# The order of two-expert and three-expert passes in a mixture-of-experts round

## The chip, the cores and the metric

The kernel runs on one core of one Trainium2 chip. The metric is the device time of one execution in microseconds (us). Times of the kernel before: 1380.34, 1383.5 and 1382.48 us, median 1382.48 us.

## What is computed

One inference step of a trunk of two layers over 256 tokens (128 context tokens, 128 latent tokens) of width 1024. Layer 0 mixes tokens with a bidirectional gated recurrence, layer 1 with differential attention; each is followed by a mixture of experts with 64 experts of width 256, of which each token takes 8. Everything is float32. The part that the change touches, cut from the reference:

```python
def moe(x, router, router_bias, w_gate, w_up, w_down, ws_gate, ws_up, ws_down):
    scores = jax.nn.sigmoid(x.astype(jnp.float32) @ router.astype(jnp.float32))
    ...
    h = jax.nn.silu(jnp.einsum('btd,edf->btef', x, w_gate)) * jnp.einsum('btd,edf->btef', x, w_up)
    routed = jnp.einsum('btef,efd->btd', h * combine[..., None].astype(x.dtype), w_down)
    shared = (jax.nn.silu(x @ ws_gate) * (x @ ws_up)) @ ws_down
    return routed + shared
```

What is left out picks 8 of the 64 experts for each token (within 4 of 8 groups); combine holds their weights and is zero elsewhere.

## The kernel before

**Passes.** Tokens are gathered per expert. A pass works on 128 rows of gathered tokens, cut into four blocks of 32. `SUBS` (line 60) says which of the pass's experts each block belongs to: kind A has two experts of 64 rows, kind B three (64, 32, 32), kind D two (96, 32). The experts are ranked by how many tokens chose them; `column_ranks` (line 67) gives three-block places to the fullest, two-block places to the middle, one-block places to the emptiest. There are 26 passes in a layer: passes 0 and 1 (kind A, experts 0 to 3) and three rounds of eight, whose kinds `BODY` (line 54) spells out: 2 + 3 x 8 = 26 passes and 4 + 3 x 20 = 64 experts. "Expert n" here means the n-th in the order of the passes.

**One pass on TensorE** (`one_pass`, from line 1343): `gate_up` (128 rows against the gate and up projections, all of the pass's experts side by side on the array), the first half of the scatter of the pass before, the turning of the hidden rows, the second half of that scatter, the gather for the next pass, `down` (hidden rows against the down projections, called here the down products), and `turn_slots` for the next pass. Passes 4, 11 and 19 carry in addition a piece of the shared expert. Pass 25, the last, takes gate and up apart: first the gate half, then both scatters, then the up half, then its down products. After it, layer 0 sums mod_w columns (`sum_mod(16)`), which needs a load of its own.

**Weights.** An expert has three loads: gate and up (1 MB each) and down (1 MB). Gate and up go into one of six places (`GATE_SLOTS`, line 50), expert n into place n mod 6; down into one of five (`DOWN_SLOTS`), expert n into place n mod 5. In the profile's names, places 0 to 3 are in `ring`, the others in `W`. Which load may follow which pass is set by two lists (lines 469 and 470):

```python
GATES_FREED = [[n + GATE_SLOTS for n in experts_of(p) if n + GATE_SLOTS < E] for p in range(PASSES)]
DOWNS_FREED = [[n + DOWN_SLOTS for n in experts_of(p) if n + DOWN_SLOTS < E] for p in range(PASSES)]
```

**The queue of loads.** SyncE issues all of them, in this order for every pass (`refill`, line 577; the first pass and the last three experts, whose gate and up are split, are left out here):

```python
eng.wait_ge(s.gu_done, done)
for n, e in gates:
    load_gate_up(gate_place(n % GATE_SLOTS), a["moe_w_gate"][L, e], a["moe_w_up"][L, e], gate_loaded(n))
eng.wait_ge(s.down_done, 2 * done)
for n, e in expert_ids(DOWNS_FREED[p]):
    load_down(down_place(n % DOWN_SLOTS), a["moe_w_down"][L, e], sem[f"down{n % DOWN_SLOTS}_loaded"])
```

So the gates that pass p frees are loaded once its gate and up products are done (line 554), the downs that it frees once its down products are done (line 557), and SyncE goes on to pass p+1 only then. On TensorE, line 1199 waits for the gate and up loads of the pass, line 1208 for its down loads.

Of the kernel before, what the change touches and what calls it, by code (L numbers as in the profile page):

```python
# [50 lines left out]
GATE_LOADS = (E - RING) // GATE_SLOTS + 1  # L51
DOWN_LOADS = (E - RING) // DOWN_SLOTS + 1
STATIC = GATE_SLOTS
BODY = "ABABABDB"
ROUNDS = 3
PASSES = 2 + ROUNDS * len(BODY)
COLS = 4 * PASSES
ITEMS = COLS + 2 * XITEMS
SUBS = {"A": (0, 0, 1, 1), "B": (0, 0, 1, 2), "D": (0, 0, 0, 1)}
FIRST = [sum(SUBS[q][-1] + 1 for q in BODY[:i]) for i in range(len(BODY))]  # L60
PER_ROUND = sum(SUBS[q][-1] + 1 for q in BODY)

# [4 lines left out]
def column_ranks():  # L67
# [3 lines left out]
    lanes = [[(0, 2), (1, 2)], [(2, 2), (3, 2)]]  # L71
    n_mid = ROUNDS * (BODY.count("B") + 2 * BODY.count("A")) - (STATIC - RING)
    small = iter(range(STATIC + ROUNDS + n_mid, E))
    for _ in range(ROUNDS):
        for kind in BODY:
            if kind == "A":
# [131 lines left out]
def trunk(nc, a, outs, gains):  # L208
    y_prompt, y_sample, new_state, new_k, new_v = outs
    ctx = ExitStack()  # L210
    with ctx:
# [240 lines left out]

        ID_COL = [4 * i + SUBS[kind].index(q) for i, kind in enumerate(BODY) for q in range(SUBS[kind][-1] + 1)]

# [2271 lines left out]
```

## Time and profile before

| | |
|---|---|
| median of three runs | 1382.48 us |
| profiled execution | 1381.2 us |
| its span, first to last instruction | 1379.4 us |
| TensorE busy | 1292.3 us (94%) |
| VectorE, ScalarE, GpSimd busy | 465.6, 342.4, 18.4 us |
| mean granted clock of TensorE | 0.984 |
| bytes moved | 507.89 MB, mean 368 GB/s |
| chain that ended last | TensorE 69%, DMA 22% |

The span is the profiler's record of one execution; the execution's own time is 1.8 us longer. Busy times are of the whole span; two stages with different limits alternate in it (mixer of layer 0, experts of layer 0, mixer of layer 1, experts of layer 1), so a share over the span says little of one stage. "Chain" is the chain of waits, followed back from the last instruction to what released each step. In rows of engines, "x32" is the number of instructions, and what stands in brackets is the idle time before the first and what ended it.

### The profile page before, as it was taken

What the parts mean: (1) busy time and instruction counts of PE and PEld (TensorE: products, weight loads), DVE (VectorE), ACT (ScalarE), POOL (GpSimd) and SP (SyncE); (2) the same over time, 40 slices, a digit from 0 to 9 for tenths busy, and PEclk for the clock granted to TensorE, in tenths of its full rate; (3) what the DMA queues carried; (4) which work ended last, traced back from release to release, by engine and by line L of the source; (5) the groups of instructions that cost most, each with busy time, mean ns of one, the idle gap of its engine ahead of it and who ended that gap; (6) DMA issues with size and microseconds to landing.
All of it is one profiled execution on the core that took longest, in us unless ns stands there. A gap on an engine that the chain in (4) does not pass through costs nothing.

```text
span 1379.4 us, 24072 instructions
## 1 busy us (share of the span) xinstructions
PE 1292.3 (94%) x9563; PEld 664.9 (48%) x9613; DVE 465.6 (34%) x1185; ACT 342.4 (25%) x695; POOL 18.4 (1%) x23
## 2 busy tenths in 40 slices
PE   7989999999999988989989999999999998998995
PEld 5757547444444433444434554644544444443442
DVE  2557534323232222222231363542223222222223
ACT  2167032212221211212131243422122122111122
POOL 2100000000000000000000000000000000000000
PEclk9999999999999999999999999999999999999999
DMA  9896899899999999999998465999999999999993
GB/s 348 216 368 246 329 368 368 337 399 408 420 420 421 421 421 420 420 420 421 416 388 298 165 218 183 364 373 399 403 420 421 420 420 421 420 420 420 420 420 146
DMA packets 114508, 507.89 MB, mean 368 GB/s; under 512 B 19036, under 2 KB 27424, under 8 KB 64352
## 3 DMA queue, kind: packets, MB, share of 16 engines
q1 hardware_dynamic: 113136, 503.42, 91.3%
q0 software_dynamic: 1008, 2.45, 0.6%
q8 instruction: 79, 1.29, 0.4%
q10 hardware_dynamic: 256, 0.49, 0.1%
q14 instruction: 29, 0.24, 0.0%
HBM read 504.18 MB, written 2.14 MB: 367 GB/s over the span
## 4 chain that ended last, share of the span: by engine, by line
PE 69%; DMA 22%; DVE 4%; ACT 2%; SPq 2%; issue 2%; ACTq 0%; DVEq 0%
PE PS L854 67%; DMA ring<-in_moe_w_up 13%; DMA W<-in_moe_w_up 6%; DMA W<-in_mod_w 2%; SPq L554 1%; DVE W L2165 1%; DMA ring<-in_mod_w 1%; PE PS L1145 1%; DVE hT L2010 0%; PE PS L862 0%; PE PS L1471 0%; ACT W L1744 0%; ACT W L1743 0%; DVE W L2162 0%; DVE diag L2032 0%
## 5 line engine op out<-in xcount | busy, mean ns | idle before, releaser
L854 PE MATMUL PS<-ring,W 128*32 128x512 f32 (+5 forms) x3112 | 582.9, 576 | 25.0 <-DMA W<-in_moe_w_up 13.2
L854 PE MATMUL PS<-W 128*128 128x128 bf16 (+7 forms) x3114 | 482.5, 367 | 12.8 <-DMA ring<-in_moe_w_up 6.9
L854 PEld LDWEIGHTS PS<-ring,W 128*32 128x32 f32 (+2 forms) x3112 | 180.0, 121 | 242.7 <-issue 228.1
L854 PEld LDWEIGHTS PS<-W 128*128 128x128 bf16 (+4 forms) x3114 | 224.1, 111 | 137.0 <-issue 126.8
L854 PE MATMUL PS<-W,junk 128*128 128x128 bf16 x848 | 116.7, 219 | 0.0
L2296 DVE TENSOR_TENSOR diag<-PS,diag 128x512 f32<-128x512 f32 x100 | 69.2, 692 | 139.3 <-ACT diag L1798 139.3
L854 PE MATMUL PS<-ring,hT 128*128 128x512 f32 x256 | 114.4, 596 | 0.8 <-issue 0.5
L2273 DVE SCALAR_TENSOR_TENSOR W<-W,PS 128x256 f32<-128x256 f32 x52 | 25.0, 480 | 261.7 <-ACT W L1785 261.7
L2290 DVE COPY W<-PS 128x512 f32<-128x512 f32 x53 | 36.7, 692 | 221.3 <-PE PS L854 221.3
L854 PE MATMUL PS<-diag,W 128*128 128x512 bf16 (+2 forms) x374 | 101.3, 394 | 8.9 <-issue 7.8
L1798 ACT CAST diag<-PS 128x512 bf16<-128x512 f32 x100 | 58.5, 585 | 190.9 <-PE PS L854 190.9
L1785 ACT ACTIVATE W<-PS 128x256 f32<-128x256 f32 x52 | 19.9, 383 | 326.3 <-PE PS L854 326.3
L854 PE MATMUL PS<-hT,ring 128*128 128x256 f32 x352 | 81.4, 389 | 2.2 <-DVE hT L2010 2.2
L854 PEld LDWEIGHTS PS<-hT,ring 128*128 128x128 f32 x352 | 67.0, 194 | 18.1 <-issue 6.7
L854 PEld LDWEIGHTS PS<-ring,hT 128*128 128x128 f32 x256 | 47.0, 190 | 55.1 <-issue 54.1
L854 PEld LDWEIGHTS PS<-diag,W 128*128 128x128 bf16 (+2 forms) x424 | 38.7, 103 | 72.0 <-issue 47.3
L854 PEld LDWEIGHTS PS<-W,junk 128*128 128x128 bf16 x848 | 67.1, 98 | 11.7 <-issue 0.6
L1793 ACT COPY W<-PS 128x512 f32<-128x512 f32 x53 | 31.0, 585 | 136.4 <-PE PS L854 136.4
L2301 DVE TENSOR_TENSOR rows<-diag 128x1024 bf16<-128x1024 f32 x50 | 61.3, 1226 | 7.7 <-ACT diag L1800 7.7
L1800 ACT CAST diag<-diag 128x1024 bf16<-128x1024 f32 x50 | 52.3, 1045 | 37.9 <-DVE diag L2296 37.9
L854 PE MATMUL PS<-rows,W 128*128 128x512 bf16 x200 | 59.5, 379 | 0.0
L854 PE MATMUL PS<-ring,condT 128*32 128x512 f32 (+1 forms) x400 | 43.9, 563 | 0.1
(278 smaller groups left out, 836.8 us busy)
## 6 DMA issues: line engine op xcount, KB each, us to landing
ring<-in_moe_w_down SPq DMA_DIRECT2D x104, 1024.0 KB, 24.3
ring<-in_moe_w_gate SPq DMA_DIRECT2D x88, 1024.0 KB, 21.0
ring<-in_moe_w_up SPq DMA_DIRECT2D x88, 1024.0 KB, 24.0
W<-in_moe_w_gate SPq DMA_DIRECT2D x41, 1024.0 KB, 20.5
W<-in_moe_w_up SPq DMA_DIRECT2D x41, 1024.0 KB, 24.1
W<-in_moe_w_down SPq DMA_DIRECT2D x25, 1024.0 KB, 23.6
ring<-in_mod_w SPq DMA_DIRECT2D x28, 768.0 KB, 9.1
ring<-in_mod_w SPq DMA_DIRECT2D x16, 1024.0 KB, 10.7
```

Source lines behind the costliest of these rows:

```text
L554: eng.dma_start(v[:, i, :], w.rearrange("(p k) f -> p (k f)", p=P)).then_inc(done, 16)
L854: return eng.matmul(out, lhsT, rhs, start=first, stop=last, skip_group_check=True)
L1145: ins = eng.transpose(PS[:, 7, fc * P:(fc + 1) * P], hE[:, fc * P:(fc + 1) * P], ident)
L1785: eng.activation(sg, PS[:, 6, 0:F], ACT.Silu).then_inc(sg_.silu_ready, 1)
L1793: eng.copy(xg[:, 0:4, :].rearrange("p k n -> p (k n)"), PS[:, 6, :]).then_inc(sg_.xg_act, 1)
L1798: eng.copy(oparts[0][:, half * 512:(half + 1) * 512], PS[:, 4 + half, :]).then_inc(sg_.o_act, 1)
L1800: eng.copy(oparts[1], orest).then_inc(sg_.o_act, 1)
L2165: ins = eng.scalar_tensor_tensor(out=y, in0=xpad[:, c, :, t:t + P], scalar=conv_w(t, c), in1=y, op0=ALU.mult, op1=ALU.add)
L2273: eng.scalar_tensor_tensor(out=hE.rearrange("p (c q) -> p c q", c=2), in0=sg.rearrange("p (q c) -> p c q", c=2), scalar=wslot[:, 0:1], in1 ...
L2290: eng.tensor_copy(xg[:, 4:8, :].rearrange("p k n -> p (k n)"), PS[:, 7, :]).then_inc(sg_.xg_dve, 1)
L2296: eng.tensor_tensor(orest[:, cols], PS[:, 4 + half, :], oparts[0][:, cols], ALU.subtract)\
L2301: eng.tensor_tensor(oparts[2], orest, oparts[1], ALU.subtract).then_inc(sg_.o_dve, 1)
```

## The change

One string, the kinds of the eight passes of a round, is written in another order. It holds three A, four B and one D as before.

```diff
-BODY = "ABABABDB"
+BODY = "ABBBAADB"
```

All tables that follow from it change with it: which experts a pass takes, which loads a pass frees, the column of each expert in the plan. Experts per pass in a round: 2, 3, 2, 3, 2, 3, 2, 3 before; 2, 3, 3, 3, 2, 2, 2, 3 now. In the last round (experts 44 to 63):

| pass | 18 | 19 | 20 | 21 | 22 | 23 | 24 | 25 |
|---|---|---|---|---|---|---|---|---|
| before | A 44-45 | B 46-48 | A 49-50 | B 51-53 | A 54-55 | B 56-58 | D 59-60 | B 61-63 |
| now | A 44-45 | B 46-48 | B 49-51 | B 52-54 | A 55-56 | A 57-58 | D 59-60 | B 61-63 |

VectorE, ScalarE and GpSimd have the same instructions in the same order. On two engines rows move.

SyncE, layer 0, the refill that follows pass 20 (waits in brackets; W and ring are the places of the weights; TENSOR_LOAD reads an expert's number). Before:

```order
L554 ISA [waits gu_done]
L554 DMA ring<-in_moe_w_gate 128x2048
L554 DMA ring<-in_moe_w_up 128x2048
...
L554 DMA ring<-in_moe_w_gate 128x2048
L554 DMA ring<-in_moe_w_up 128x2048
L568 TENSOR_LOAD W [waits down_done]
...
L557 DMA W<-in_moe_w_down 128x2048
...
L557 DMA ring<-in_moe_w_down 128x2048
```

Now:

```order
L554 ISA [waits gu_done]
L554 DMA ring<-in_moe_w_gate 128x2048
L554 DMA ring<-in_moe_w_up 128x2048
...
L554 DMA ring<-in_moe_w_gate 128x2048
L554 DMA ring<-in_moe_w_up 128x2048
...
L554 DMA ring<-in_moe_w_gate 128x2048
L554 DMA ring<-in_moe_w_up 128x2048
L568 TENSOR_LOAD W [waits down_done]
...
L557 DMA W<-in_moe_w_down 128x2048
...
L557 DMA ring<-in_moe_w_down 128x2048
...
L557 DMA ring<-in_moe_w_down 128x2048
```

Pass 20 now frees three places of each kind instead of two: a third gate and up pair goes out behind its gate_up (expert 57's), and a third down load (expert 56's) behind its down products; the refill of pass 21, which had three of each, still has three.

TensorE, layer 1, passes 19, 20 and 21: the first product of each group with what it waits for (slotN_loaded is gate and up place N, downN_loaded is down place N), in the order down products of 19, gate_up and down products of 20, gate_up and down products of 21. Before:

```order
L854 MATMUL PS<-ring,W 32x512 [waits down2_loaded,down3_loaded,down1_loaded,hT_ready]
...
L854 MATMUL PS<-ring,W 64x512 [waits slot0_loaded,slot1_loaded,xg_dve,xg_act]
...
L854 MATMUL PS<-W 64x512 [waits down0_loaded,down4_loaded,hT_ready]
...
L854 MATMUL PS<-ring,W 32x512 [waits slot3_loaded,slot2_loaded,slot4_loaded,xg_dve,xg_act]
...
L854 MATMUL PS<-ring,W 32x512 [waits down2_loaded,down3_loaded,down1_loaded,hT_ready]
```

Now:

```order
L854 MATMUL PS<-ring,W 32x512 [waits down2_loaded,down3_loaded,down1_loaded,hT_ready]
...
L854 MATMUL PS<-ring,W 32x512 [waits slot2_loaded,slot1_loaded,slot3_loaded,xg_dve,xg_act]
...
L854 MATMUL PS<-W 32x512 [waits down0_loaded,down1_loaded,down4_loaded,hT_ready]
...
L854 MATMUL PS<-W 32x512 [waits slot5_loaded,slot4_loaded,slot0_loaded,xg_dve,xg_act]
...
L854 MATMUL PS<-ring,W 32x512 [waits down3_loaded,down4_loaded,down2_loaded,hT_ready]
```

Before, the down places of neighbouring passes are 1, 2, 3, then 0, 4, then 1, 2, 3. Now they are 1, 2, 3, then 0, 1, 4, then 2, 3, 4: pass 20 waits for place 1, which pass 19 used, and pass 21 for place 4, which pass 20 used. The gate and up places of neighbouring passes have none in common in either order.

## Rows read from the trace of the kernel before

**Rows 1.** The page: TensorE's line, and what DMA moved in 40 slices of 34.5 us

```profile
PE 1292.3 (94%) x9563; PEld 664.9 (48%) x9613; DVE 465.6 (34%) x1185; ACT 342.4 (25%) x695; POOL 18.4 (1%) x23
...
GB/s 348 216 368 246 329 368 368 337 399 408 420 420 421 421 421 420 420 420 421 416 388 298 165 218 183 364 373 399 403 420 421 420 420 421 420 420 420 420 420 146
```

**Rows 2.** Windows: stretch, length, busy us per engine, PEclk, DMA share, GB/s

```profile
290.00:688.00 398.00, 375.82 (x3242) 175.37 (x3261) 109.88 (x242) 78.00 (x132) 0.00 (x0) 0.99 1.01 419
951.00:1348.00 397.00, 376.95 (x3233) 174.37 (x3252) 109.88 (x242) 77.27 (x130) 0.00 (x0) 0.98 1.01 419
312.00:324.00 12.00, 12.00 (x120) 5.35 (x121) 5.03 (x11) 2.80 (x4) 0.00 (x0) 1.00 0.97 382
```

**Rows 3.** Chain, first scatters of passes 6 to 8: start us, us, what

```profile
341.85 1.24 PE PS L854 x5
...
358.28 1.24 PE PS L854 x5
...
374.70 1.24 PE PS L854 x5
```

**Rows 4.** Timeline of TensorE, layer 1, passes 23 to 25: start us, us, instruction

```profile
1316.54 3.64 PE L854 MATMUL PS<-ring,W 128*32 128x512 f32 x32
...
1320.38 0.62 PE L854 MATMUL PS<-ring,W 128*32 128x512 f32 x1
...
1332.98 0.62 PE L854 MATMUL PS<-ring,W 128*32 128x512 f32 x1
...
1336.78 3.66 PE L854 MATMUL PS<-ring,W 128*32 128x256 f32 x64
1340.60 0.81 PE L854 MATMUL PS<-diag,W 128*128 128x512 bf16 x3 [0.16 <-DMA ring<-in_moe_w_up]
...
1348.65 3.64 PE L854 MATMUL PS<-ring,W 128*32 128x512 f32 x32 [0.46 <-ACT W L1789]
```

**Rows 5.** Timeline of TensorE, layer 0, pass 25 and what follows it

```profile
675.77 3.66 PE L854 MATMUL PS<-ring,W 128*32 128x256 f32 x64
...
688.18 3.64 PE L854 MATMUL PS<-ring,W 128*32 128x512 f32 x32 [1.00 <-DMA ring<-in_moe_w_down]
691.75 3.70 PE L854 MATMUL PS<-diag,W 128*128 128x512 f32 x8
699.01 3.64 PE L854 MATMUL PS<-W,condT 128*32 128x512 f32 x16 [3.56 <-issue]
```

**Rows 6.** Line 557 (down loads), 270:380 us, then 400:690 us

```profile
DMA to landing us min/median/max: 6.2/13.6/20.0
...
DMA to landing us min/median/max: 21.7/26.5/29.6
```

**Rows 7.** Chain: gates of passes 15, 17, 24; mod_w; pass 23 of layer 1

```profile
491.33 7.11 PE PS L854 x64
...
528.58 9.80 PE PS L854 x64
...
659.31 7.11 PE PS L854 x64
...
667.94 28.02 DMA W<-in_mod_w
695.97 3.05 issue
...
1302.43 8.58 PE PS L854 x64
```

**Rows 8.** Timeline of all engines, end of pass 10 in layer 0

```profile
416.51 0.23 PE L854 MATMUL PS<-both,W 128*128 128x128 bf16 x1
...
417.89 0.34 SPq L557 DMA_DIRECT2D W<-in_moe_w_down  x1
```

**Rows 9.** Windows in the gate products of pass 17 (layer 0), pass 23 (layer 1)

```profile
528.50:530.50 2.00, 1.92 (x12) 0.68 (x16) 0.51 (x2) 0.00 (x0) 0.00 (x0) 0.50 1.04 434
1302.40:1311.10 8.70, 8.58 (x64) 2.51 (x66) 0.86 (x2) 0.02 (x1) 0.00 (x0) 0.82 1.01 422
```

## The prediction

> **What bounds the kernel now.** The page first. TensorE is busy 94% of the span, and the core's DMA engines move 420 GB/s in two long stretches of slices [rows 1]. The windows put edges on those stretches: 290 to 688 us (layer 0's experts) and 951 to 1348 us (layer 1's) run at 419 GB/s with a DMA share of 1.01 [rows 2]. An expert is three loads of 1.049 MB (gate, up, down), so a load takes 1.049 MB / 419 GB/s = 2.50 us, and an expert 7.5 us. Next TensorE's own pace, from the chain of waits in a stretch where no pass waits for a load: the first scatters of passes 6, 7 and 8 (kinds A, B, D) stand 16.43 and 16.42 us apart, two experts or three alike [rows 3]. A round of eight passes is 20 experts: 150 us of DMA against 131 us of TensorE. So once the lead of the first passes is used up, DMA sets the pace, and TensorE waits for up projections ahead of its three-expert passes.
>
> The end of each stage is read from TensorE's timeline. In layer 1 the last wait of any length ends at 1302.4 us (expert 58's up projection, pass 23) [rows 7]; from there to pass 25's start at 1336.8 us TensorE runs unbroken [rows 4]. So a stage ends "the last late load, plus the TensorE passes still to run". What comes after the last pass hangs on TensorE alone in layer 1; in layer 0 TensorE ends at 691.75 + 3.70 = 695.45 us and goes on at 699.01 us, just after a load of mod_w landed at 695.97 us [rows 5, 7].
>
> **The change, part by part.** *Work.* Every layer still has 64 experts, three A, four B and one D in a round, the same sizes in the same classes, the same bytes. A pass costs TensorE 16.42 us whatever its kind [rows 3]. Nothing is added or removed: 0 us. VectorE and ScalarE have the same instructions in the same order.
>
> *Gate and up loads.* There are six places for them. A pass of three frees three and the next takes the other three, so B after B still finds its gates in flight: no new wait. In the first round pass 4 frees three places instead of two, and the third pair of loads goes out one pass earlier. DMA ran at 382 GB/s there for 12 us [rows 2]; filling that gives at most 1.1 us a layer. I take 0: the end is set much later, by the sum below, and this gain is within its bounds.
>
> *Down loads, where the change bites.* There are only five places. In the old order neighbours hold 2+3 or 3+2 experts, so a pass's down projections are always in other places than its predecessor's. In B after B (passes 4, 5, 12, 13, 20, 21) six are wanted: the third expert's down projection can be issued only when the pass before has finished its own. What time is there? The issue comes 1.4 us after the last down product (417.89 us, against 416.51 us, when the turning of the next slots begins right behind it) [rows 8]. The next down products start 1332.98 - 1316.54 = 16.44 us after the previous ones, which run 3.64 us [rows 4]. So the load has 16.44 - 3.64 - 1.4 = 11.4 us. From issue to landing, down loads took 6.2 to 20.0 us, median 13.6, in the first round, and 21.7 to 29.6, median 26.5, after 400 us [rows 6], since by then some ten loads (26.5 / 2.5) are in front of them or their own. So in rounds 2 and 3 two passes each stall in front of their down products, on passes 12, 13, 20 and 21.
>
> *Where it reaches the end.* The stream itself does not stop: when a stalled down load lands, eight loads are still queued (20 us) and the next issue follows 3.6 + 1.4 us later. So the stream's end stays: layer 0's last down load lands at 688.1 us, because pass 25 waits for it [rows 5]. In layer 1 the last up load lands at 1340.5 us [rows 4] and three down loads follow, 1340.5 + 7.5 = 1348.0 us. I count back from there. In the new order the load that pass 21 stalls on, expert 54's down, is the first of pass 20's down refills. Behind it come 2 more of them, 6 + 3 of pass 21, 4 + 2 of pass 22, 2 + 2 of pass 23: 21 loads. The spacing near the end is (1340.6 - 1302.4) / 15 = 2.54 us in layer 1 (15 loads from up 58 to up 63 in the old order) and (688.2 - 659.3) / 11 = 2.62 us in layer 0 [rows 4, 5, 7]; with the 2.50 us of the windows I take 2.55. So expert 54's down lands at 688.1 - 53.6 = 634.5 us and 1348.0 - 53.6 = 1294.4 us.
>
> From there TensorE alone counts, since passes 22, 23 and 24 hold two experts each (15 us of loads against 16.42). Down products and turns take 3.84 us to the next gate product (1320.38 - 1316.54) [rows 4], then three passes, 49.3 us: pass 25 starts at 687.6 and 1347.5 us. It started at 675.77 and 1336.78 us [rows 4, 5]. **Plus 11.8 us in layer 0, plus 10.7 us in layer 1.** In layer 0 pass 25 no longer waits for its last down load (1.00 us idle before those products, 0.46 in layer 1 where the load was there), so 0.5 us comes back: 11.3. In words: in layer 1 the old order has two passes, 23 and 24, between its last late load and pass 25; the new one has three, because the stall moves ahead of the two A passes.
>
> *TensorE's clock.* Gate products behind a wait for a load took 7.11 us in some passes and 8.58 to 9.80 us in others; there 0.50 (1.2 GHz) was granted for the first 2 us, or 0.82 on the mean, half of the full 2.4 GHz and then all of it [rows 7, 9]. The stall of pass 21 is longer: its gate starts at 634.5 - 9 x 2.55 + 3.84 = 615.4 us, its down products are ready 12.6 us later at 628.0, so it waits 6.5 us. The price is 0 (7.11 us, no drop) to 2.7 us (9.80 us); I take 1.5 (8.58), the value in the last such pass of layer 1, per layer. The Trainium skill, page "TensorE: Matmul & The Clock Gate", section "HAM oscillation — how this bites in real kernels", has it that a matmul group that waits for DMA starts again at the low clock, each time. By it every stall pays and the sum is as below; by the rows alone, where 7.11 us also stands behind a wait, it would be 3.0 us less.
>
> *After layer 0.* The mod_w load now lands before TensorE is done (it only follows the stream). If the 3.56 us from 695.45 to 699.01 belong to TensorE's branch, all 12.8 us pass on; if they hung on that load, up to 3.4 of them vanish. The row says "issue", not a wait [rows 5, 7], so I take all. Layer 1 then begins that much later and repeats the pattern.
>
> **Sum:** (11.3 + 1.5) + (10.7 + 1.5) = +25.0 us. The profiled execution took 1381.2 us (span 1379.4), 1.3 us under the median of 1382.48, so 1382.5 + 25.0 = **1407.5 us**.
>
> **Bounds.** Clock 0 to 2.7 each: -3.0 to +2.4. Load spacing 2.62 or 2.50 over 21 loads: -2.9 to +2.1. Mod_w: -3.4. Landings out of turn by one load a layer: -5 to +5. All low ends together 1393, all high ends 1417; they will not meet.
>
> **Rivals.**
> *The late down load is not late (other side).* If a down load landed within the 11.4 us it has, B after B would cost nothing. Then pass 21 starts with expert 54's up, 31 loads before the end: 609.0 us, and four passes later pass 25 at 674.8, against 675.8 before; only up 63 stands one place nearer to the stream's end, 2.5 us later, which I carry with +1 us: 1383.5. For it: 6.2 us and a median of 13.6 in the first round [rows 6]. Against it: never under 21.7 after 400 us. It decides at 11.4 us. The Trainium skill, "DMA: Bandwidth & Descriptors", section "Bandwidth", gives 6.15 us for a transfer of 1 MB; by that figure alone the load would be in time. The trace agrees for a queue that is nearly empty, and differs wherever ten loads stand ahead. Chance 0.05.
> *Only one layer pays.* Layer 0's delay is caught up in the attention stage, where DMA is ahead: 1382.5 + 12.2 = 1394.7. Against: the chain there is TensorE and the normalisations. Chance 0.06.
> *The clock stays low through the whole down product:* 3.6 us more instead of 1.5, and again on the first gate product behind: about 1413. Chance 0.12.
> *The queue runs dry.* SyncE waits in order, for down_done, with the gates of the next pass behind; if the 20 us in front of it were less than the 6 it is held, each layer would lose 5 us of stream: 1417. Chance 0.05.
> *The change does not reach the loads.* Excluded by the order of SyncE's instructions.
>
> **How the numbers follow.** Forecast 0.72. Range 1396 to 1414 us: it leaves out the first rival, part of the second, the queue that runs dry, and the tails of the bounds. About 0.2% (2.8 us) is what a measurement can tell from no change. Slower by more: 0.72 + 0.12 + 0.05 + 0.06 less a little for errors of the whole count, 0.94; within: 0.05; faster: 0.01 (only the 1.1 us a layer of the first round speaks for it).
>
> **What would show it.** TensorE's waits for in_moe_w_down, now one of 1.0 us at the end of layer 0 [rows 5], become some 50 to 65 us, eight of them of 4 to 11 us, ahead of 128x512 down products; the waits for in_moe_w_up shrink to little. DMA stays at 419 GB/s to about 688 us, pass 25 starts near 688 us (689 with the clock), and layer 1's last four passes run without a wait. Wrong would be: the stream's end moved, no waits for down loads, or passes 22 to 25 waiting for up projections.

## The result, and the profile after

The changed kernel takes 1408.15 us (median of 4 runs, 1406.83 to 1409.43), the kernel before 1382.99 us on the same chip (4 runs, 1380.34 to 1383.74): a ratio of 1.0178, 95% interval 1.0165 to 1.0192, so 25.2 us more. The prediction was 1407.5 us, in a range of 1396 to 1414. The profiled execution took 1407.52 us, its span 1405.6 us, 26.2 us longer than the span before. Below, "before" means the kernel before, and "A", "B", "D" are the kinds of passes.

The page of the changed kernel, with the lines that answer to [rows 1], its waits for weights by the page's groups, and its chain by engine:

```profile
span 1405.6 us, 24120 instructions
...
PE 1307.5 (93%) x9613; PEld 661.1 (47%) x9613; DVE 465.8 (33%) x1185; ACT 342.9 (24%) x695; POOL 18.4 (1%) x23
...
GB/s 349 223 362 253 328 370 346 353 404 419 421 420 420 421 421 420 421 420 421 363 315 280 156 210 194 365 367 405 419 420 420 421 421 420 420 421 421 420 335 65
...
PE 82%; DMA 10%; DVE 4%; ACT 2%; issue 1%; SPq 1%; ACTq 0%; DVEq 0%
```

The two long stretches at 420 GB/s are still there and no slice in them is lower: the stream of weights did not pause. But the chain is now 82% TensorE and 10% DMA, where it was 69% and 22%. That sounds like a kernel that DMA holds up less, and it is 25 us slower. TensorE now runs unbroken through more passes behind its last wait in each stage, so its own pace, and no longer the stream's, sets when the stage ends.

The windows of the changed kernel (columns as in [rows 2]):

```profile
290.00:688.00 398.00, 372.16 (x3133) 168.09 (x3130) 106.56 (x234) 75.95 (x128) 0.00 (x0) 0.97 1.01 420
...
312.00:324.00 12.00, 12.00 (x135) 5.68 (x137) 5.19 (x11) 2.81 (x4) 0.00 (x0) 1.00 1.01 417
```

The dip of the first round is filled, 417 GB/s where it was 382 [rows 2]: the third pair of gate and up loads does go out one pass earlier.

Waits of the changed kernel (engine, line, what it waited for: us in total, times, longest):

```profile
PE PS L854 <- DMA ring<-in_moe_w_down: 35.8, 4, 9.9
...
PE PS L854 <- DMA W<-in_moe_w_down: 14.2, 4, 3.8
```

Eight waits, 50.0 us together, two in each of the last two rounds of each layer. No wait for in_moe_w_up is left among the long ones; before, these were 17.0 + 15.1 us. Here are the last two of layer 0 and of layer 1 on TensorE's timeline of the changed kernel, each ahead of down products (128x512), with the gate products of the pass behind (passes 20, 21 and 22; then the same in layer 1):

```profile
611.80 1.07 PE L854 MATMUL PS<-W 128*32 128x512 f32 x2 [8.01 <-DMA ring<-in_moe_w_down]
...
617.96 0.62 PE L854 MATMUL PS<-ring,W 128*32 128x512 f32 x1
...
634.15 1.07 PE L854 MATMUL PS<-ring,W 128*32 128x512 f32 x3 [3.55 <-DMA W<-in_moe_w_down]
...
639.36 7.09 PE L854 MATMUL PS<-ring,W 128*64 128x512 f32 x32
...
1284.62 1.07 PE L854 MATMUL PS<-W 128*32 128x512 f32 x2 [8.26 <-DMA ring<-in_moe_w_down]
...
1306.99 1.07 PE L854 MATMUL PS<-ring,W 128*32 128x512 f32 x3 [3.77 <-DMA W<-in_moe_w_down]
...
1313.69 7.09 PE L854 MATMUL PS<-ring,W 128*64 128x512 f32 x32
```

The first number in brackets is the wait, the landing of the load ends it. The single products take 1.07 us where the same form takes 0.62 elsewhere: the clock has fallen. And the chain of the changed kernel from pass 20's stall to the end of layer 0, with what follows in both layers:

```profile
592.83 18.84 DMA ring<-in_moe_w_down
...
619.64 14.38 DMA W<-in_moe_w_down
634.15 13.69 PE PS L854 x74
...
648.06 16.23 PE PS L854 x112
...
664.51 16.21 PE PS L854 x144
...
680.94 17.72 PE PS L854 x230
...
707.81 3.71 issue
...
1306.99 15.18 PE PS L854 x74
...
1322.40 16.23 PE PS L854 x112
...
1338.84 16.21 PE PS L854 x144
```

From 634.15 us on, three steps of 16.4 us of TensorE alone. Pass 25's first gate product stands at 688.67 us and at 1363.00 us; before, at 675.77 and 1336.78 us [rows 4, 5]. The changed kernel reaches the experts of layer 0 (the first gate product of pass 0) 0.87 us later and those of layer 1 13.19 us later, so pass 25 itself lost 688.67 - 675.77 - 0.87 = **12.0 us** in layer 0 and 1363.00 - 1336.78 - 13.19 = **13.0 us** in layer 1. These two are the whole loss of the span but for 1.2 us, most of it the 0.87 that stood there before any expert ran.

In what follows, "pass 25 moved by" is such a number: where the pass stands, against before, with the start of its layer's experts laid on each other.

### The profile page after: what moved, and what is told of

Its sections match the earlier page's. It is cut to its first block, busy times and chain, and to the rows that moved or that the text cites. A ratio compares the mean times of both kernels' runs of the same rounds, so it can differ in the third digit from the quotient of the medians.

```text
span 1405.6 us, 24120 instructions
## 1 busy us (share of the span) xinstructions
PE 1307.5 (93%) x9613; PEld 661.1 (47%) x9613; DVE 465.8 (33%) x1185; ACT 342.9 (24%) x695; POOL 18.4 (1%) x23
## 4 chain that ended last, share of the span: by engine, by line
PE 82%; DMA 10%; DVE 4%; ACT 2%; issue 1%; SPq 1%; ACTq 0%; DVEq 0%
PE PS L854 79%; DMA ring<-in_moe_w_down 6%; DMA W<-in_moe_w_down 4%; DVE W L2165 1%; PE PS L1145 1%; SPq L568 1%; PE PS L862 0%; DMA rows<-in_norm_g 0%; PE PS L968 0%; DVE hT L2010 0%; PE PS L1471 0%; ACT W L1744 0%; ACT W L1743 0%; DVE W L2162 0%; DVE diag L2032 0%
## 5 line engine op out<-in xcount | busy, mean ns | idle before, releaser
L854 PE MATMUL PS<-ring,W 128*32 128x512 f32 (+5 forms) x3064 | 602.9, 581 | 15.1 <-DMA W<-in_moe_w_down 14.2
L854 PE MATMUL PS<-W 128*128 128x128 bf16 (+7 forms) x3162 | 504.4, 374 | 41.9 <-DMA ring<-in_moe_w_down 35.8
L854 PE MATMUL PS<-diag,W 128*128 128x512 bf16 (+2 forms) x424 | 112.5, 393 | 1.0 <-DVE diag L2542 1.0
```

Source lines behind the costliest of these rows:

```text
L854: return eng.matmul(out, lhsT, rhs, start=first, stop=last, skip_group_check=True)
```

## The experiments

My theory: B after B wants six down places where five are, so a down load is issued late; that load's place in the stream is fixed, and the end of a layer is its landing plus the TensorE passes still to run. What matters is where the last such load stands. Rivals: any stall costs what it lasts, wherever it stands; it is the grouping of the experts (fewer, larger refills, a fuller or emptier queue) and not the number of places; it is the clock that each stall leaves behind. Medians of the kernel before were 1383.97 us beside the first four kernels, and 1382.94 us beside the last four.

### The new order in the last round alone, and in the first two alone

Rounds may differ: `BODY` becomes three strings, and the lists made from it are taken per round.

```diff
-BODY = "ABABABDB"
+BODIES = ('ABABABDB', 'ABABABDB', 'ABBBAADB')
...
-    for _ in range(ROUNDS):
-        for kind in BODY:
+    for body in BODIES:
+        for kind in body:
```

> Rounds 1 and 2 of each layer in the old order (ABABABDB), only the last round in the new one (ABBBAADB). My theory (only a stall whose place in the stream is followed by TensorE-bound passes to the end counts): all of the loss is there, ratio to before 1.016 to 1.020, 1405 to 1411 us, with two waits for in_moe_w_down per layer (passes 20 and 21). Rival (every stall in front of down products adds its length): four of eight stalls are gone, about half the loss, 1394 to 1397 us.

Measured: 1413.0 us (1411.66 to 1413.6), ratio 1.0209 (1.0190 to 1.0228), 29.0 us more than before. Pass 25 moved by 14.7 and 13.9 us.

The other way round, with 'ABBBAADB' twice and 'ABABABDB' last:

> Rounds 1 and 2 in the new order, the last round in the old one. My theory: the stalls of passes 12 and 13 (about 10 and 4 us, in both layers) are still there, and cost nothing, since DMA sets the end; the first round's fuller queue gives 0 to 1 us a layer: 1380 to 1384 us. Rival (every stall adds): 1394 to 1397 us.

Measured: 1383.48 us (10 runs, 1378.76 to 1384.76), ratio 0.9996 (0.9987 to 1.0006). Pass 25 moved by -0.9 and -1.7 us. The stalls of passes 12 and 13 were there all the same, 9.7 and 3.4 us in layer 0 and 9.7 and 3.7 us in layer 1; the other two waits for places in `ring` are 1.0 us each, ahead of pass 25's down products:

```profile
PE PS L856 <- DMA ring<-in_moe_w_down: 21.5, 4, 9.7
PE PS L856 <- DMA W<-in_moe_w_down: 7.1, 2, 3.7
...
PE PS L856 <- DMA ring<-in_moe_w_up: 4.4, 4, 1.5
```

Pass 14 of layer 0 stood 17.0 us late behind the stalls of passes 12 and 13, and pass 21 only 0.6 us. A stall of 10 us with DMA at work throughout costs nothing here: the loads go on landing behind it, and the waits for up projections, 17.0 + 15.1 us in the kernel before, shrink to 4.4 + 1.1 us. So "a stall costs what it lasts" is out: the same edit costs all of it in the last round and none of it in the first two.

The first kernel, though, loses 3 to 4 us more than the change, 2 us past what I had allowed. Its timeline shows one more long wait, ahead of pass 20's gate products:

```profile
591.08 8.48 PE L856 MATMUL PS<-ring,W 128*32 128x512 f32 x64 [6.29 <-DMA ring<-in_moe_w_up]
...
613.69 1.07 PE L856 MATMUL PS<-W 128*32 128x512 f32 x2 [8.53 <-DMA ring<-in_moe_w_down]
...
636.05 1.08 PE L856 MATMUL PS<-ring,W 128*32 128x512 f32 x3 [3.82 <-DMA W<-in_moe_w_down]
```

In layer 0, pass 25 moved by 14.7 us, 2.7 more than in the change. Expert 54's down is at hand at 636.05 us; this kernel's experts start 0.69 us later than those of the change, where on this clock it would be 634.15 + 0.69 = 634.8 us. So 1.2 us is a later landing, about what the dip of the first round is worth, which this kernel doesn't fill. The rest is the clock behind the stall, which stays low for longer: the next gate products are at 642.68 us, 6.63 us behind the start of the down products (granted clock 0.52 from 636.05 to 642.00 us), where the change needs 639.36 - 634.15 = 5.21 us (0.73 over these):

```profile
642.68 7.09 PE L856 MATMUL PS<-ring,W 128*64 128x512 f32 x32
```

In layer 1 pass 25 moved by 0.9 us more than in the change. By the count, the wait of 6.29 us has no term of its own: the stall ends when its load lands, whatever came before.

### A sixth place for down projections, under both orders

Under the new order this takes away the cause and leaves the grouping. The kernel has one tile of the size of a load that holds gate and up of the shared expert until pass 11 (`ggb`); from round 2 on it can be a sixth down place. `DOWN_AT` writes out the place of each expert (n mod 5 first, six in turn from expert 26 to 55, the last three where their halves are expected).

```diff
-BODY = "ABABABDB"
+BODY = "ABBBAADB"
...
+        DOWN_AT = [0, 1, 2, 3, 4, 0, 1, 2, 3, 4, 0, 1, 2, 3, 4, 0, 1, 2, 3, 4, 0, 1, 2, 3, 4, 0, 5, 1, 2, 3, 4, 0, 5, 1, 2, 3, 4, 0, 5, 1, 2, 3, 4, 0, 5, 1, 2, 3, 4, 0, 5, 1, 2, 3, 4, 0, 1, 2, 3, 4, 0, 1, 2, 3]
...
-            return ring[:, q, 4096:6144] if q < RING else place4[:, 4096:6144]
+            return ring[:, q, 4096:6144] if q < RING else place4[:, 4096:6144] if q == RING else ggb_down
```

> The new order, with a sixth place for down projections from round 2 on (the 8 KB a partition that the shared expert's up projection has left). My theory (the stalls come from five places for six experts): no wait for in_moe_w_down above 2 us, 1382 to 1391 us; a few us may remain, since down loads are issued earlier and push gate loads back. Rival (it is the grouping itself: three big passes in a row, then three small ones that TensorE cannot finish before the end): no gain from the place, 1404 to 1410 us.

Measured: 1389.89 us (6 runs, 1387.81 to 1394.01), ratio 1.0041 (1.0026 to 1.0056). Its waits:

```profile
PE PS L868 <- DMA ring<-in_moe_w_up: 29.8, 11, 4.3
PE PS L868 <- DMA W<-in_moe_w_up: 4.5, 2, 2.8
...
PE PS L868 <- DMA ring<-in_moe_w_down: 0.7, 1, 0.7
```

The stalls on down loads are gone, and of the 25.2 us only 5.9 are left: the five places carry 19 us (17, if the control below is taken as the base). The 5.9 are a second, smaller price of the grouping; the expectation allowed for a few us, as gate loads pushed back, and the theory had no count for it. The last long wait of layer 1 is now this one:

```profile
1278.18 9.82 PE PS L868 x64
```

It is the gate of pass 21, waiting 3.47 us for expert 54's up projection, and four passes follow it, where before the last long wait (expert 58's up, ahead of pass 23) had two behind it [rows 7]. In layer 1 it is the same law with another load: three B in a row reach further ahead in the stream than the alternation does, and the two A behind them give back a lead that nothing uses. I read this from the rows; no run takes the two A passes away. Layer 0 does not fit it: passes 20 to 22 wait as well, and pass 25 itself waits for a gate load, which the kernel before does not do:

```profile
681.93 3.66 PE L868 MATMUL PS<-ring,W 128*32 128x256 f32 x64 [1.10 <-DMA ring<-in_moe_w_gate]
```

That load comes late in the stream itself; what pushes it back there stays open. Pass 25 moved by 3.8 and 4.2 us, 8.0 together, in a profiled execution of 1394.01 us, the longest of the six.

As a control, the same six places with the old order:

> Control: the old order with the same sixth place. Both theories: no change, 1381 to 1385 us; a gain over 3 us would mean that the sixth place does something else than take the stalls away.

Measured: 1381.92 us (10 runs, 1380.3 to 1383.68), ratio 0.9984 (0.9974 to 0.9994). The sixth place gives the old order at most a quarter of a per cent, so the 19 us above were not saved by the place as such. Layer 1 shows where a gain of this size can sit. Pass 23's gate products start behind next to no wait and their single products take 0.63 us, where before they waited 2.95 us and took 8.58 us in all [rows 7]; the last wait for an up projection is now 0.89 us ahead of pass 24:

```profile
1304.15 0.63 PE L868 MATMUL PS<-ring,W 128*32 128x512 f32 x3
...
1321.53 0.63 PE L868 MATMUL PS<-W 128*32 128x512 f32 x3 [0.89 <-DMA ring<-in_moe_w_up]
```

### The same neighbours at the end of the round, and one pair instead of two

If the position of the last late down load is what counts, B after B as the last two passes should be free: there the stalls of rounds 1 and 2 are swallowed, and in round 3 nothing is queued behind the last loads.

```diff
-BODY = "ABABABDB"
+BODY = "ABABADBB"
```

> All rounds in the order ABABADBB: B after B again, once a round, but as the last two passes. My theory (a down load is late only where the queue in front of it is long, and counts only where TensorE-bound passes follow): in the last round nothing is queued any more when the load goes out, it needs some 6 us of its 11.4, so there is no stall in passes 24 and 25; the stall of passes 16 and 17 (5 to 10 us) is swallowed. 1381 to 1388 us. Rival (every B after B costs): four stalls in place of none, some 1395 us.

Measured: 1382.36 us (10 runs, 1380.24 to 1384.1), ratio 0.9993 (0.9984 to 1.0002). Pass 25 moved by -0.1 and +0.2 us, with two stalls a layer in the rounds before (3.7 and 8.9 us, then 3.7 and 8.6 us):

```profile
PE PS L854 <- DMA ring<-in_moe_w_down: 24.9, 4, 8.9
PE PS L854 <- DMA ring<-in_moe_w_up: 6.9, 3, 3.4
```

The outcome was as expected, the figure behind it was not: the load that pass 25 waits for took 10.5 us from issue to landing in layer 0 and 9.8 us in layer 1, not some 6. In layer 0 it went out at 678.0 us and was there at 688.5, and the down products began at 689.21 us. So there was no stall, with 0.7 us to spare.

With one pair in the middle (passes 19 and 20 are B, then A, B, A, D, B, wait for it at pass 20):

```diff
-BODY = "ABABABDB"
+BODY = "ABBABADB"
```

> All rounds in the order ABBABADB: one B after B per round, in passes 4, 12 and 20, in place of two. My theory, by counting: expert 51's down load has 30 loads behind it, as in the new order, so it lands 76 us before the stream's end, and five passes later (down products 3.8 us, 2.3 us of clock, 4 x 16.43 us) pass 25 starts some 6.5 us a layer later than before: 1394 to 1400 us. Rival (only two stalls in a row leave a debt): 1383 to 1388 us.

Measured: 1395.64 us (1394.77 to 1397.95), ratio 1.0095 (1.0080 to 1.0109), 12.7 us more. Pass 25 moved by 7.2 and 5.9 us. The timeline of this kernel has pass 20's stall in both layers, and none behind it of any length:

```profile
612.41 1.06 PE L854 MATMUL PS<-W 128*32 128x512 f32 x2 [8.01 <-DMA ring<-in_moe_w_down]
...
1279.42 1.07 PE L854 MATMUL PS<-W 128*32 128x512 f32 x2 [7.02 <-DMA ring<-in_moe_w_down]
```

Note what this says of adding up, in layer 0. The stall of pass 20 alone (8.01 us) costs 7.2 us. With pass 21's stall of 3.55 us behind it, in the change, the cost is 12.0 us, more than 7.2 + 3.6. What fits both is when the last stall ends and how many passes follow: from 612.41 us to pass 25 at 684.40 us here, from 634.15 to 688.67 us in the change.

### The clock kept up through the stalls

The kernel has a helper that issues transposes whose result nobody reads. With it the stalls of passes 12, 13, 20 and 21 are filled in part, ahead of the down products; the order is the new one.

```diff
+                    keep_clock(4, {12: 60, 13: 32, 20: 56, 21: 36}.get(p, 0))
                     pass_down(p)
```

> The new order, with junk transposes in front of the down products of passes 12, 13, 20 and 21 (60, 32, 56, 36 of them), short enough to fit into the stalls, so that TensorE is busy while it waits. My theory: the down products of pass 21 run at the full clock (3.64 us instead of 5.0 and 6.5 us), which is on the path to the end: 4 us less than the new order, 1402 to 1406 us. Rival (what the clock costs is hidden behind the loads): 1406 to 1410 us. If the junk is longer than a stall, it costs its excess.

Measured: 1405.33 us (1402.01 to 1408.93), ratio 1.0169 (1.0153 to 1.0185). Pass 25 moved by 10.7 and 10.6 us, where in the change it was 12.0 and 13.0. Windows over the down products of passes 20 and 21 in layer 0, then the same in layer 1 (columns as in [rows 9]):

```profile
610.80:616.80 6.00, 5.93 (x56) 2.00 (x60) 2.21 (x7) 2.06 (x3) 0.00 (x0) 1.00 1.02 423
633.20:638.00 4.80, 4.75 (x42) 1.69 (x44) 1.13 (x2) 1.17 (x2) 0.00 (x0) 1.00 1.01 422
1281.70:1287.70 6.00, 5.99 (x44) 1.76 (x48) 0.75 (x2) 1.17 (x2) 0.00 (x0) 0.72 1.02 422
1304.30:1309.00 4.70, 4.67 (x40) 1.66 (x42) 1.04 (x2) 1.17 (x2) 0.00 (x0) 1.00 1.01 420
```

Where the clock was kept, the stall's tail is gone: these windows show 1.00 behind pass 21 in both layers (pass 20's in layer 1 shows 0.72, so it was not kept everywhere). The medians say 2.8 us less than the change, the two passes 25 say 1.3 + 2.4 = 3.7. The intervals of the two ratios overlap, so by the times alone a gain is likely and not settled; the granted clocks are clear. The clock as the main cause is out: with it kept, 22.4 us of the loss remain.

### The version most likely to win

Six places from round 2, and the new order in the first round alone, where it fills the dip:

```diff
-BODY = "ABABABDB"
+BODIES = ('ABBBAADB', 'ABABABDB', 'ABABABDB')
```

> Six places for down projections, first round in the new order, the other two in the old one. My theory: the fuller queue of the first round (the stream ends about 1 us earlier in each layer) and shorter gate waits at the end add up to 1 to 3 us: 1379 to 1383 us, at or just under the kernel before. Rival (the stream's end leaves nothing to gain): no difference from the kernel before.

Measured: 1382.54 us (12 runs, 1379.47 to 1385.16), ratio 0.9995 (0.9986 to 1.0005): no difference. In the profiled execution (1383.34 us) the gain does reach pass 25, which moved by -1.2 and -2.0 us (-0.2 and -0.6 us in the control), and is lost behind it. Pass 25 of layer 1 now waits 0.95 us for its last down load, and the 88 products from there on take 11.66 us, at a granted clock of 0.85 in 1349.0 to 1360.6 us, where before they took 9.96 us at 1.00. And in the mixer of layer 1 a stretch of 33 products takes 9.38 us at 0.67 (814.4 to 823.8 us), where before it took 6.43 us at 1.00. The kernel above with the new order in the first two rounds also fills the dip; it has the same gain at pass 25 (-0.9 and -1.7 us) and not the loss in the mixer, and its profiled execution is the shortest of all, 1378.76 us; its median is no lower either. So the dip is worth a microsecond or two a layer up to pass 25, and the swings of the clock are as large. No version here beats the old order by more than the 0.16% of the sixth place alone.

## Why the prediction was right

**The count held.** The sum was 25.0 us, the medians say 25.2. By layer, pass 25 was to start 11.8 + 1.5 = 13.3 us and 10.7 + 1.5 = 12.2 us later, and moved by 12.0 and 13.0 us. The core of the count was to place expert 54's down load by counting 21 loads of 2.55 us back from the stream's end. It was to land at 634.5 us and, with the 13.19 us that layer 1 starts later, at 1294.4 + 13.2 = 1307.6 us. It landed at 619.64 + 14.38 = 634.0 us, which is 633.2 on the clock of the kernel before, and at 1306.9 us: 1.3 and 0.7 us early.

**The first round was worth something after all.** I took 0 of at most 1.1 us a layer. Pass 25's last down load landed at 687.77 us, 686.9 without the late start, against 688.1: the whole 1.1 us. So the step "this gain is within its bounds" was taken at the wrong end. My argument for 0, that the end is set later, does not agree with my own count: that goes back from the stream's end, and what moves that moves all. Layer 1's landing came 0.7 us early, too, and the kernel that does not fill the dip has expert 54's down 1.2 us later.

**The clock.** I took 1.5 us a layer, out of 0 to 2.7. From the down products to the next gate products the changed kernel needs 639.36 - 634.15 = 5.21 us in layer 0 and 1313.69 - 1306.99 = 6.70 us in layer 1, against 3.84 [rows 4]: 1.37 and 2.86 us. The windows of the changed kernel show it:

```profile
611.80:615.90 4.10, 4.10 (x20) 1.12 (x24) 0.00 (x0) 0.40 (x1) 0.00 (x0) 0.50 1.01 422
634.10:638.30 4.20, 4.15 (x28) 1.32 (x32) 0.16 (x1) 0.59 (x1) 0.00 (x0) 0.66 1.02 425
638.30:646.60 8.30, 8.30 (x48) 2.52 (x38) 3.65 (x9) 1.74 (x3) 0.00 (x0) 1.00 1.01 419
1306.90:1312.00 5.10, 5.00 (x24) 1.36 (x28) 0.69 (x1) 0.59 (x1) 0.00 (x0) 0.50 1.02 422
```

In layer 1 it lasts for 5.1 us at 0.50 (1.2 GHz), in layer 0 for a part of 4.2 us; the gate products behind are at full clock. The term was too small by 1.2 us over both layers, and the landings came 2.0 us early over both, so the two errors nearly cancel. That the total came out within 1 us is luck to that extent. The Trainium skill (page "TensorE: Matmul & The Clock Gate", section "HAM oscillation — how this bites in real kernels") tells of a kernel in which every group of matmuls behind a wait for DMA starts at the low clock again. All eight stalls here agree, 3.37 to 9.89 us long: their first products take 1.07 us. The kernel before does not agree throughout: on its timeline two gates stand behind waits of the same length, the one of pass 15 at full clock, the one of pass 17 not [rows 7]:

```profile
491.33 7.07 PE L854 MATMUL PS<-ring,W 128*32 128x512 f32 x64 [3.36 <-DMA ring<-in_moe_w_up]
...
528.58 1.07 PE L854 MATMUL PS<-W 128*32 128x512 f32 x2 [3.37 <-DMA ring<-in_moe_w_up]
```

**What the stall of pass 21 lasted.** Predicted 6.5 us, measured 3.55 and 3.77. The step that failed was "its gate starts at 615.4": pass 20's load was at hand at 611.80 as counted (634.5 - 9 x 2.55 = 611.6), but pass 20's down products ran at half clock too, 617.96 - 611.80 = 6.16 us to the next gate instead of 3.84. Those 2.3 us came out of pass 21's wait. I had named the price and forgotten to charge it to the stall ahead. It changes no sum, since the load's landing ends that wait either way. The eight waits add up to 50.0 us, at the low edge of the 50 to 65 that I gave, and span 3.4 to 9.9 us, not 4 to 11.

**Issue to landing.** The load had 11.4 us and I set it against a median of 26.5 us [rows 6]. In the changed kernel line 557 shows this between 400 and 700 us:

```profile
  PE PS L854: 24.6, 4
...
DMA to landing us min/median/max: 11.9/18.4/25.8
```

Expert 54's down took 14.38 us, only 3 us more than it had. The stalls of TensorE hold SyncE back, so fewer loads lie ahead of each: in the kernel with the same order, six places and hardly a stall, the median over 400 to 690 us is 26.0 us, as before. The time in the queue got shorter by a third, and the stream never ran dry. The threshold of the first rival was nearer than my two rows made it look, though all eight waits show that it was not reached. The Trainium skill (page "DMA: Bandwidth & Descriptors", section "Bandwidth") gives 6.15 us for 1 MB, as the busy time of the DMA engines for a load issued from GpSimd. By it the load would have been in time; the trace decides against it, with 14.38 us in this queue.

**After layer 0.** The whole delay passed on: the "issue" stretch behind pass 25 is 3.71 us, where it was 3.56 [rows 5]. Taking all of it was right, and "only one layer pays" was not. Of the 0.5 us that pass 25's missing wait was to give back in layer 0, 0.4 came: from pass 25's first gate product to the first of `sum_mod` it took 699.01 - 675.77 = 23.24 us before and 711.52 - 688.67 = 22.85 us after.

**The rivals.** The late down loads were late (each of the eight waits is 3.37 us or longer); both layers paid; the clock was low for most of one down product in layer 1 alone; the queue stayed at 420 GB/s.

**What the prediction had as one cause is two.** It explained 25 us by five places. With six places 5.9 us remain; in layer 1 the last long wait, then for an up projection, has four passes behind it instead of two, and for layer 0 the cause is open. In the real change the down stall comes later and covers this, as I read it. The forecast did not need it, but the sentence "no new wait" for gate and up loads would have misled anybody who wanted to save the order by adding a place.

## What to carry to other kernels

Where a stream of loads is the bound, a stage ends at "the last late load, plus the compute behind it". List the passes behind the last wait, before and after the edit, and count the loads from there to the stream's end; the length and the number of stalls in between matter little (stalls of up to 9.7 us in earlier rounds cost nothing here). When passes of different size share a ring of buffers, the ring must hold the largest sum of neighbours, and where it doesn't, put such neighbours where no stream follows them; even with the sixth place this order cost 5.9 us. And a higher share of TensorE in the chain is not a better kernel: here it rose from 69% to 82% with 25 us lost.

## What was not expected of the hardware

The price of a wait in clock varied at nearly equal length: waits of 3.55 and 3.77 us ahead of the same products cost 1.37 and 2.86 us, one of 3.36 us before gate products cost nothing and one of 3.37 us cost 2.7 us (9.80 against 7.11). No row tells what decided it. Second, the time from issue to landing depends on what stands ahead of a load: with TensorE stalled for 50 us in all, the median of the down loads fell from 26.5 to 18.4 us at the same 420 GB/s, and without the stalls, in the same order, it was 26.0 us. Third, where the queue is long the issuing itself takes time: the issue of an up projection (line 554, places in `ring`, 400 to 690 us) held SyncE for 2.07 us in the median and up to 6.2 us in the kernel before, and 0.38 us in the median in the changed one (to 700 us); the loads of that line took 25.9 and 21.4 us from issue to landing in the median.
